# Two-layer diffusion trunk step on one core: expert weights loaded during the output projection, a fused last choice in the router's tail, gathers that read their list directly, and unread matrix products in TensorE's waits

## The reference

```python
x = post_norm(x, concat([ya, yb, yc]) @ w_out[l], g_a, ln_g[l, 0], ln_b[l, 0])
h = x * (1.0 + sc_f) + sh_f
x = post_norm(x, moe_ffn(h, w_router_grp[l], w_router_exp[l], w_e_gate[l], w_e_up[l], w_e_down[l]),
              g_f, ln_g[l, 1], ln_b[l, 1])
# moe_ffn: the group with the largest of 4 logits, in it the 2 largest of 8 expert logits,
# y = sum over the two of weight * ((silu(h @ w_g[e]) * (h @ w_u[e])) @ w_d[e]), 32 experts in all
```

## Time and profile before

| | us |
|---|---|
| median of 3 runs (1667.3 to 1669.96) | 1669.04 |
| the profiled execution | 1667.84 |
| its span | 1666.0 |
| PE busy in the span | 1448.5 |
| DVE busy in the span | 617.1 |
| POOL busy in the span | 391.9 |

### The profile page before, as it was taken

How to read it: one execution, slowest core, us unless ns; L and a number is a source line. 1 busy time by engine, 2 the same in 40 slices (tenths; PEclk the granted TensorE clock), 3 DMA queues, 4 the chain that set the end, 5 groups by cost and what they waited for, 6 DMA issues and landing times.

```text
span 1666.0 us, 23079 instructions
## 1 busy us (share of the span) xinstructions
PE 1448.5 (87%) x8501; PEld 997.3 (60%) x8501; DVE 617.1 (37%) x1454; ACT 351.7 (21%) x908; POOL 391.9 (24%) x537
## 2 busy tenths in 40 slices
PE   6999999997993899897799999999697569899764
PEld 4889889675882333342288989967477434333321
DVE  1301333765458121111351133466728742121116
ACT  2111112654000111111141121156400101111103
POOL 1000032623534111111110001453256221211110
PEclk8999999999995999999899999999998779999987
DMA  9321112875209899999621111176130679999954
GB/s 368 96 69 61 35 56 74 285 260 197 91 26 377 326 369 421 396 412 361 250 85 61 60 61 61 35 276 241 40 127 26 265 286 382 415 413 420 383 226 163
DMA packets 75758, 356.26 MB, mean 214 GB/s; under 512 B 21152, under 2 KB 24480, under 8 KB 40832
## 3 DMA queue, kind: packets, MB, share of 16 engines
q1 hardware_dynamic: 41184, 291.58, 44.5%
q0 software_dynamic: 21888, 48.83, 8.2%
q10 hardware_dynamic: 12576, 14.37, 2.6%
HBM read 344.37 MB, written 33.12 MB: 227 GB/s over the span
## 4 chain that ended last, share of the span: by engine, by line
PE 70%; DMA 18%; DVE 5%; issue 3%; POOL 2%; ACT 1%; SPq 1%; ACTq 0%; POOLq 0%; DVEq 0%
PE bank L978 24%; PE bank L1319 11%; DMA att<-h_rows,cur 9%; PE bank L1204 7%; PE bank L1338 4%; DMA ring<-in_w_exp 4%; PE bank L727 2%; PE bank L758 2%; PE bank L1303 2%; PE bank L1130 2%; PE bank L1104 2%; DMA z<-in_w_ada 1%; PE bank L742 1%; PE bank L935 1%; DMA att<-bias_full 1%
## 5 line engine op out<-in xcount | busy, mean ns | idle before, releaser
L978 PE MATMUL bank<-ring,hT 128*128 128x256 f32 (+1 forms) x1920 | 411.4, 374 | 2.4 <-ACT hT L1430 2.4
L978 PEld LDWEIGHTS bank<-ring,hT 128*128 128x128 f32 x1920 | 353.3, 191 | 47.4 <-issue 2.9
L1319 PE MATMUL bank<-ring,att 128*64 128x512 f32 (+1 forms) x448 | 186.3, 647 | 3.3 <-DMA z<-in_w_exp 3.3
L1319 PE MATMUL bank<-z,att 128*64 128x512 f32 (+1 forms) x416 | 164.2, 618 | 16.0 <-DMA ring<-in_w_exp 16.0
L1204 PE MATMUL bank<-ring,hT 128*128 128x256 f32 x640 | 145.8, 388 | 7.3 <-DMA ring<-in_w_out 5.8
L1204 PEld LDWEIGHTS bank<-ring,hT 128*128 128x128 f32 x640 | 123.1, 195 | 24.2 <-issue 7.6
L2347 DVE TENSOR_TENSOR att<-att,bank 128x256 f32<-128x256 f32 x38 | 16.0, 421 | 294.9 <-ACT att L1670 294.9
L1319 PEld LDWEIGHTS bank<-ring,att 128*64 128x64 f32 (+1 forms) x448 | 60.7, 162 | 82.1 <-issue 82.1
L1319 PEld LDWEIGHTS bank<-z,att 128*64 128x64 f32 (+1 forms) x416 | 52.7, 151 | 74.7 <-issue 74.7
L2635 POOL COPY cur<-att 128x1 int32<-128x1 int32 (+1 forms) x38 | 6.9, 182 | 377.5 <-ACT att L1677 280.2
L1303 PE MATMUL bank<-const,att 128*128 128x128 f32 x320 | 48.1, 299 | 54.6 <-DMA att<-h_rows,cur 54.6
(11 more groups left out here) (366 smaller groups left out, 2168.9 us busy)
## 6 DMA issues: line engine op xcount, KB each, us to landing
ring<-in_w_exp SPq DMA_DIRECT2D x84, 1024.0 KB, 16.8
z<-in_w_exp SPq DMA_DIRECT2D x78, 1024.0 KB, 17.8
ring<-in_w_ada SPq DMA_DIRECT2D x41, 1024.0 KB, 5.5
ring<-in_w_in SPq DMA_DIRECT2D x24, 1024.0 KB, 4.9
hT<-in_w_exp SPq DMA_DIRECT2D x20, 1024.0 KB, 15.7
att<-in_w_exp SPq DMA_DIRECT2D x10, 1024.0 KB, 14.8
z<-expert_rows ACTq DMA_DIRECT2D x20, 512.0 KB, 8.2
ring<-in_w_out SPq DMA_DIRECT2D x8, 1024.0 KB, 8.4
```

What stands on the lines that cost most here:

```text
L978: last = eng.matmul(bk[:, i * UN:i * UN + nw], hTv[:, k, t * P:(t + 1) * P], w[:, k, 0:nw], start=(k == 0), stop=(k == KD - 1))
L1319: last = eng.matmul(bank[2 + j][c * m_:(c + 1) * m_, :], e["xT"][:, j, k * P + c * m_:k * P + (c + 1) * m_], wv[c][:, :, k, :], start=(k = ...
```

## The change

- **Loads.** SP loads the four first experts in twelve pieces. Five are issued at `ld_scsh`, when the projection has begun: the ring slots that held no unit of w_out, and three parts of `z` that nothing uses. The four slots of w_out follow as they come free, two pieces come after the last residual, one after the last logits. Before it waits for `ctl`, SP now waits until the gathers 0 and 1 have landed. The rows `ln2` take the place of `free` in `z`, and GpSimd's temporary moves to `hs`.
- **Projection.** `project` waits for each unit of w_out on its own instead of for all four.
- **Router's tail.** `choose_last` replaces `choose(1)` for the single last tile, with the compare fused with its multiply: 15 instructions up to `assign`, not 19, and the two that feed ACT come after it. DVE adds the shift to the last two tiles (`rows_shifted`). ACT clears `xg`. `ranks(0)` moves ahead of the last transposes.
- **Gathers.** In the fixed passes the gather takes its column of `gidx` itself, without the copy to `cur` and the wait for it; in pass 0 gate and up come before the transposes of pass 1, on all three engines.
- **Unread products.** `keep_busy(n)` issues n products of 128 by 128 by 128 that nothing reads, at four places: 16, 26, 22 and 36 in each layer.

Waits between DVE's own instructions in `choose_last` and the reordered passes of ACT and DVE are left out below.

```diff
--- before.py
+++ after.py
@@ -458,14 +458,13 @@
-            ("ln", P, 2, D), ("free", P, 2, D), ("ga", P, 2, D)])
+            ("ln", P, 2, D), ("ln2", P, 2, D), ("ga", P, 2, D)])
...
-        m["ln2"] = region(z, 2048 + 3 * KD * UN, P, 2, D)
@@ -662,18 +661,29 @@
-                for n in range(2):
-                    for q in range(3):
-                        eng.wait_ge(*ev.at(*holder[3 * n + q]))
-                    gate_up(n, lambda q: A["w_exp"][l, n, q])
-                    down(n, lambda q: A["w_exp"][l, n, q])
+                def piece(n, q):
+                    into, landed = (wdn[n], f"wd{n}") if q == 2 else (wgu[n][:, q, :], f"wgu{n}")
+                    eng.dma_start(into, A["w_exp"][l, n, q]).then_inc(W[landed], 16)
+
+                with_out = [s for s in range(RING) if holder[s][2] == "out"]
+                eng.wait_ge(*ev.at("ld_scsh", l))
+                for s in range(RING):
+                    if s not in with_out:
+                        eng.wait_ge(*ev.at(*holder[s]))
+                        piece(s // 3, s % 3)
+                for n, q in ((2, 2), (3, 0), (3, 1)):
+                    piece(n, q)
+                for s in with_out:
+                    eng.wait_ge(*ev.at(*holder[s]))
+                    piece(s // 3, s % 3)
                 eng.wait_ge(*ev.at("u", l, NT - 1))
                 eng.wait_ge(*ev.at("rows", l))
-                for n in range(2, 4):
-                    if n == 3:
-                        eng.wait_ge(*ev.at("full", jobs.number(("RL", l, NT - 1))))
-                    gate_up(n, lambda q: A["w_exp"][l, n, q])
-                    down(n, lambda q: A["w_exp"][l, n, q])
+                piece(2, 0)
+                piece(2, 1)
+                eng.wait_ge(*ev.at("full", jobs.number(("RL", l, NT - 1))))
+                piece(3, 2)
+                for j in range(2):
+                    eng.wait_ge(W[f"gath{j}"], 16)
                 eng.wait_ge(*ev.at("ctl", l))
@@ -747,6 +757,11 @@
+            def keep_busy(n):
+                for _ in range(n):
+                    eng.matmul(ada_ps[:, 0:P], ident, K["ones"], start=True, stop=True)
@@ -1197,8 +1212,11 @@
-                w = [unit_view((l, "out", u)) for u in range(N_OUT)]
+                w = {}
                 def project(t, half, i):
+                    if t == 0:
+                        w[2 * half + i] = unit_view((l, "out", 2 * half + i))
                     bk = jobs.bank("Y", l, t, half)
@@ -1261,9 +1279,11 @@
+                ranks(0)
                 rows_turned(NT - 1)
-                ranks(0)
                 logits(NT - 1)
+                eng.wait_ge(*(ev.at("hcol", l + 1) if l + 1 < DEPTH else ev.at("modT", l, 1)))
+                keep_busy(16)
                 ranks(1)
@@ -1277,6 +1297,7 @@
+                keep_busy(26)
                 bk = jobs.open("RX", l)
@@ -1349,15 +1370,21 @@
                 def one_pass(b_):
-                    block_x(b_ + 1)
-                    block_gu(b_)
+                    if isinstance(b_, int) and b_ == 0:
+                        block_gu(b_)
+                        block_x(b_ + 1)
+                    else:
+                        block_x(b_ + 1)
+                        block_gu(b_)
                     if above_zero(b_):
                         block_down(b_ - 1)
                     block_hT(b_)
+                keep_busy(22)
                 block_x(0)
                 n = passes(eng, l, one_pass)
                 block_down(n - 1)
+                keep_busy(36)
@@ -1652,6 +1679,12 @@
+                for t in range(NT):
+                    eng.wait_ge(*ev.at("st_h2", l, t))
+                eng.wait_ge(*ev.at("assign", l, 1))
+                for j in range(2):
+                    last = eng.activation(e["xg"][:, j, :].rearrange("p (k n) -> p k n", k=KD), bc(K["ones"], 1, KD), ACT.Copy, scale=0.0)
+                last.then_inc(*act.event("nought", l))
 
                 W = MOE[l]
...
@@ -2132,6 +2169,10 @@
+                def rows_shifted(t):
+                    hs = lr["hs"][:, t % 2, :]
+                    eng.tensor_tensor(hs, hs, lr["scsh"][:, 1, min(t, 1), :], ALU.add).then_inc(*dve.event("h2", l, t))
+
@@ -2181,6 +2222,46 @@
+                def choose_last():
+                    part, t = 1, NT - 1
+                    col = lambda i: s5[:, i, t:t + 1]
+                    lg, le = r["lg"][:, t, 0:NG], r["lg"][:, t, NG:36].rearrange("p (g e) -> p g e", g=NG)
+                    tg, th, lem, hit = r["tg"][:, t, :], r["th"][:, t, :], r["lem"][:, t, :], r["t1"][:, t, :]
+                    eng.wait_ge(*jobs.empty("RL", l, t))
+                    eng.tensor_reduce(col(0), lg, AX, ALU.max).then_inc(*dve.step())
+                    eng.scalar_tensor_tensor(out=th, in0=lg, scalar=col(0), in1=K["io4"], op0=ALU.is_equal,
+                                             op1=ALU.mult).then_inc(*dve.step())
+                    eng.tensor_reduce(col(1), th, AX, ALU.max).then_inc(*dve.step())
+                    eng.tensor_scalar(th, th, col(1), -1.0, ALU.is_equal, ALU.add).then_inc(*dve.step())
+                    eng.scalar_tensor_tensor(out=lem.rearrange("p (g e) -> p g e", g=NG), in0=bc(th, 2, EPG), scalar=-NEG, in1=le,
+                                             op0=ALU.mult, op1=ALU.add).then_inc(*dve.step())
+                    def top(val, one):
+                        eng.tensor_reduce(val, lem, AX, ALU.max).then_inc(*dve.step())
+                        eng.scalar_tensor_tensor(out=hit, in0=lem, scalar=val, in1=K["io32"], op0=ALU.is_equal,
+                                                 op1=ALU.mult).then_inc(*dve.step())
+                        eng.tensor_reduce(col(5), hit, AX, ALU.max).then_inc(*dve.step())
+                        eng.tensor_scalar(one, hit, col(5), None, ALU.is_equal).then_inc(*dve.step())
+
+                    top(col(3), r["e1"][:, t, :])
+                    eng.scalar_tensor_tensor(out=lem, in0=r["e1"][:, t, :], scalar=2 * NEG, in1=lem, op0=ALU.mult,
+                                             op1=ALU.add).then_inc(*dve.step())
+                    top(col(4), r["e2"][:, t, :])
+                    eng.tensor_tensor(r["ma"][:, t, :], r["e1"][:, t, :], r["e2"][:, t, :], ALU.add).then_inc(*dve.event("assign", l, part))
+                    eng.tensor_scalar(tg, lg, col(0), None, ALU.subtract).then_inc(*dve.event("r_gd", l, part))
+                    eng.tensor_tensor(col(6), col(4), col(3), ALU.subtract).then_inc(*dve.event("r_dl", l, part))
@@ -2218,8 +2299,9 @@
                 expert_rows(NT - 2)
+                rows_shifted(NT - 2)
                 logit_rows(NT - 1)
-                choose(1)
+                choose_last()
                 expert_rows(NT - 1)
@@ -2241,6 +2323,7 @@
                 eng.tensor_reduce(kr[0:NE, 5, 0:1], kr[0:NE, 4, :], AX, ALU.add).then_inc(*dve.event("place", l))
+                rows_shifted(NT - 1)
                 bk = jobs.bank("RB", l)
                 eng.wait_ge(*jobs.full("RB", l))
...
@@ -2572,18 +2659,19 @@
                 eng.wait_ge(*ev.at("ld_scsh", l))
                 eng.wait_ge(*ev.at("ld_ln", 1, l))
                 for g in range(2):
-                    eng.tensor_tensor(m["free"][:, g, :], lr["scsh"][:, 0, g, :], m["ln"][:, 1, :], ALU.mult).then_inc(*pool.step())
+                    eng.tensor_tensor(lr["hs"][:, g, :], lr["scsh"][:, 0, g, :], m["ln"][:, 1, :], ALU.mult).then_inc(*pool.step())
                     eng.wait_ge(*pool.last())
-                    eng.tensor_tensor(lr["scsh"][:, 1, g, :], lr["scsh"][:, 1, g, :], m["free"][:, g, :], ALU.add)
+                    eng.tensor_tensor(lr["scsh"][:, 1, g, :], lr["scsh"][:, 1, g, :], lr["hs"][:, g, :], ALU.add)
                     last = eng.tensor_tensor(lr["scsh"][:, 0, g, :], lr["scsh"][:, 0, g, :], m["ln"][:, 0, :], ALU.mult)
                 last.then_inc(*pool.event("rows", l))
                 eng.wait_ge(*pool.last())
                 def store_rows(t):
-                    eng.wait_ge(*ev.at("hsc", l, t))
                     hs = lr["hs"][:, t % 2, :]
-                    eng.tensor_tensor(hs, hs, lr["scsh"][:, 1, min(t, 1), :], ALU.add).then_inc(*pool.event("h2", l, t))
-                    eng.wait_ge(*pool.last())
+                    if t < NT - 2:
+                        eng.wait_ge(*ev.at("hsc", l, t))
+                        eng.tensor_tensor(hs, hs, lr["scsh"][:, 1, min(t, 1), :], ALU.add).then_inc(*pool.event("h2", l, t))
+                    eng.wait_ge(*ev.at("h2", l, t))
                     ld(h2_dram[l][t * P:(t + 1) * P, :], hs, "st_h2", l, t, sem=f"st_h2_{t % 2}")
                 for t in range(NT):
@@ -2598,10 +2686,7 @@
                 store_rows(NT - 1)
                 for t in range(NT):
                     eng.wait_ge(*ev.at("st_h2", l, t))
-                eng.wait_ge(*ev.at("assign", l, 1))
-                eng.memset(e["xg"][:, 0, :], 0.0)
-                eng.memset(e["xg"][:, 1, :], 0.0).then_inc(*pool.step())
```

(10 more changed lines are left out.)

26 lines of the change are left out of this document (22 added, 4 removed).

## The result

The changed kernel takes 1654.9 us, the median of 6 runs (1649.17 to 1660.58), beside 1668.71 for the kernel before (6 runs, 1665.38 to 1672.75): a ratio of 0.9918, 95% interval 0.9902 to 0.9935. That is 13.8 us faster, inside the range and on the forecast side, but only half of the 28.0 us of the sum. The profiled execution of after took 1653.13 us with a span of 1651.3, and its mean granted clock rose from 0.933 to 0.953.

A forecast was written before the change was run, and what follows sets the result against it. The prediction took the stream of expert weights, started by the end of pass 0's gate and up, to set the pace. Terms 3.6 + 7.9 + 9.2 + 2.2 + 2.1 + 3.0 = 28.0 us gave 1641, range 1628 to 1657.

The forecast's parts named there:

- the moment: End of gate and up of pass 0, which starts the full weight stream; forecast 7.9 us earlier, 9.2 in layer 1.
- Projection: Start of layer 0's projection: a wait per unit of w_out brings 3.6 us, bounds 0 and 4.9; layer 1 nothing.
- The collision priced at 449.2: Layer 0's projection: transposes of tile 1 near 449.2, not 447.8, where the second residual meets GpSimd's add.
- Steps 1 to 5: Router's tail, logits to lists: shift +0.7, choice 1.3 earlier, comparison 2.7 earlier, second shift +0.3, list products 2.5 us.
- Step 6: First gather, without copy and wait, issues near 526.6; rows land 5.0 us later, transposes of pass 0 end at 532.6.
- Step 7: DVE's readout of pass 0's transposes, late through two GpSimd adds, comes at 537.0; gate and up start at 537.8.
- Step 8: Gate and up of pass 0, now ahead of pass 1's transposes, still take 8.3 us and end at 546.2.
- The stream: Expert passes behind the moment: move as a block, with 1.5 us a layer gained, bounds 0 and 6.
- Combination: Combination behind the expert passes, no longer started cold: 2.2 us in layer 0, 2.1 in layer 1, bounds 0 and 2.5.
- part of the gain is absorbed: Rival: projection's start brings 0, tail 5 a layer through new DVE and GpSimd collisions, combination waits: 1656, chance 0.22.
- Bound by the gather's latency: Rival: the expert passes are bound by gather latency, not bytes, giving 6 us a layer, not 1.5: 1632, chance 0.2.
- The slower rival: Rival: unread products run at 1.2 GHz, 0.24 us each, deciding from about 0.19 us an instruction: 1683, chance 0.05.

The follow-up runs named there:

- run 9: The kernel before, unaltered, timed and profiled again: 1667.78 us, ratio 0.9995.
- Run 4: The changed kernel with the copy to `cur` and its wait restored ahead of every gather: 1658.35 us, ratio 0.9935.
- run 5: The changed kernel with GpSimd's two layer norm additions and the loads behind them moved behind gather 2: 1643.61 us, ratio 0.9833.
- Run 7: The changed kernel with 18 more unread products behind the transposes of pass 0: 1652.38 us, ratio 0.9895.
- run 1: The changed kernel again, with no edit: 1654.62 us, ratio 0.992.
- run 3: The changed kernel with the twelve weight pieces loaded after the last projection, as before, and without SP's wait for the gathers: 1653.7 us, ratio 0.991.
- run 6: The changed kernel with GpSimd's two additions behind gather 2, and 20 and 14 unread products for 26 and 22: 1641.23 us, ratio 0.9841.
- runs 8 and 11: Changed kernel with pass 0's old order, 1656.31 us; changed kernel with GpSimd's additions behind gather 2, early loads and SP's gather wait undone, 1651.88 us.

## Why the prediction was half right

The direction and the place were right: the gain comes through the moment, and from there the work moves as a block (252.26 and 252.83 us before, 252.21 and 252.72 after). Its steps against the rows, in us from the end of layer 0's logits (505.1 in the working, 505.62 after):

| step | before | forecast | after |
|---|---|---|---|
| 2, `assign` | 5.7 | 4.4 | 4.8 |
| 3, counts compared | 9.4 | 6.7 | 6.8 |
| 4, list products start | 20.0 | 17.7 | 17.7 |
| 5, lists | 25.5 | 21.3 | 21.0 |
| 6, transposes of pass 0 end | 34.1 | 27.5 | 28.8 |
| 7, gate and up start | 40.7 | 32.7 | 33.3 |
| 8, gate and up end | 49.0 | 41.1 | 42.9 |

- **Projection.** The forecast gave 3.6 us; to the transposes of tile 1 the means of run 9 give 42.1 less 38.7, 3.4. The collision priced at 449.2 in the text came. The failed part is "behind it TensorE is without a gap, so the shift holds": in the 3.91 us of wait that the step left out TensorE loses its clock, and 2.2 us (94.5 less 92.3) reach the logits, 1.8 by the mean of eleven profiles. Run 4's profile shows what the clock costs: there the wait was 2.97 us, the granted clock stayed at 1.00 over the 7 us behind it (0.76 in after), and the stretch took 90.0, 4.5 less than before. Of the 2.4 us by which it beats after, the shorter wait is 0.9. In run 5's profile the clock was 0.56 over these 7 us, the last logits took 2.91 us instead of 1.95, and nothing was gained (95.0).
- **Steps 1 to 5** hold within 0.4 us. The second shift fits into the sums' wait, at 0, not 0.3. No stall is left in the choice and the comparison takes 0.18 us. The rule on VectorE and GpSimd that the prediction cites from the Trainium skill ("SBUF — State Buffer", section "Who interferes with whom") agrees with the rows outside the choice as well: with the additions moved, 3.71 and 2.30 us became 0.87 and 0.17.
- **Step 6** was 1.3 off, since the 22 unread products end at 533.5, not 531.0 (0.154 us each, not 0.13, and started at 526.8; the granted clock was 0.50 from 528 to 530). It cost nothing, VectorE being later still.
- **Step 7** named the collision and sized it 0.6 too small.
- **Step 8** failed in its mechanism: "they still take 8.3 us". They took 9.65 and 9.79 where 8.29 and 8.89 had stood before. The text took the colder start as priced by the row of before. There, transposes of 1.97 us stand directly ahead of gate and up and take the first of the slow time: the granted clock is 0.50 in the first 2 us of gate and up and 0.88 in the next two. After, gate and up come straight from 4.49 us of idle and have 0.50 for all four. Run 7 shows the clock as cause, since unread products in that wait bring 7.09. The size varies: gate and up behind cold transposes, with the old order of pass 0, took 7.6 to 9.2 us in eight cases. Steps 7 and 8 together leave 6.0 and 7.1 of the 7.9 and 9.2 (the terms of the 9.2 add up to 9.3).
- **The stream.** "The gather's missing copy" was to give 1.5 a layer, and gives nothing measurable: the lengths above, and run 4 in layer 1. This is the largest single term that failed, 3.0 of the 28.0 us. That a gather issued 1 us sooner waits for the same bytes is argued from the full DMA share; in part the rows agree, since from issue to landing the median gather of a window of 220 us takes 10.2 us with the copies (before, and run 4 in layer 1) and 10.5 and 10.8 without (after, run 1).
- **Combination.** 2.3 and 2.1 us by the rows of the combination; forecast 2.2 and 2.1. That both came out is partly luck. In the ten profiles with the 36 unread products, seven of twenty combinations took 12.2 us (layer 0) or 19.1 (layer 1), since the granted clock fell after their start, as in run 5, layer 0, combination from 808.24 on:

```profile
810.24:812.24 2.00, 2.00 (x4) 0.68 (x3) 1.35 (x2) 0.00 (x0) 0.00 (x0) 0.50 1.03 412
```

The terms as measured are 2.2 + 6.0 + 7.1 + 0 + 2.3 + 2.1 = 19.7 us, against 28.0. Of the 8.3 us that are missing, 3.0 are the stream's, 4.0 those of steps 6 to 8 and 1.4 the projection's; the combination gave 0.1 more than forecast. The spans of the two profiles of each kernel (1666.0 and 1664.7; 1651.3 and 1644.8) differ by 17.3 in the mean, the medians by 13.8 and 15.5. The two profiles of the changed kernel are of executions faster than its median. In the first pair of profiles, what stands between the 19.7 and the 14.7 of the spans lies mostly in attention, which the change doesn't touch: it took some 3 us more in each layer. Beyond that: runs of the changed kernel spread over 16 us, those of before over nearly 9, and the time goes with the granted clock (0.954 in runs of 1646.6 and 1649.2 us, 0.947 in runs of 1660.6 and 1662.7). Without unread products the spread is 3.3 us (five runs), but run 3, which has them, spreads over 4.2. Where clock is lost in some executions the profiles show in part: at the start of a combination (seven of twenty, 1.7 us each), in the list products (three of eighteen, 2.0 us each) and behind the wait in the projection. Why it is lost there in some executions and not in others stays open, and so does what is left between 19.7 and 13.8.

Of the rivals, "part of the gain is absorbed" (1656) came true in size, and in half of its mechanism: VectorE and GpSimd do collide anew, and moving GpSimd's additions brings 11 us. The tail didn't fall to 5 a layer nor did the combination wait. "Bound by the gather's latency" is refuted by the streams. The slower rival's condition held for part of two groups (granted clock 0.50), but no group came to its 0.19 us an instruction: they took 0.12 to 0.17 in the two profiles of the changed kernel, and without them the kernel is 5.3 us slower.

What the prediction missed most was the reach of its own step 7. It took the additions as given, "in both versions", and so did not ask what they cost once their cover was gone. Their price is 0 in the kernel before, 11 us in the changed one, and 1.8, which the intervals don't tell from none, with the loads as before.

## What to carry to other kernels

When a change removes the wait that ended last, list what else ended inside it: here two GpSimd additions of 2.4 us, free before, cost 11 us after, and the early loads for which the change was made paid (8 us) only when these were moved. Two edits that bring nothing by themselves can bring something together, so cross them. GpSimd additions that VectorE's small instructions have to sit out belong behind the gather that the critical chain needs next, not in front of it. Price a burst of TensorE by the granted clock at its start, not by its own former duration: the same 32 instructions took 7.09 to 9.87 us. The wait directly ahead isn't enough to tell that clock: after 4.49 us it was low, but in run 3 also after 0.92, behind short transposes and a longer wait.

## What the runs showed of the hardware

- VectorE instructions of one element or five columns last as long as the GpSimd addition of 128x1024 beside them (3.71 for five, 2.30 for one; 0.87 and 0.17 without it). All that an addition stretched have two tensors in SBUF as inputs. Instructions with one such input stood beside an addition too and weren't stretched. In the kernel before, the reduction directly ahead of the 4-column subtraction that took 1.34 us lies inside the same addition and takes its 0.16:

```profile
504.71 2.34 POOL L2585 TENSOR_TENSOR att<-att 128x1024 f32<-128x1024 f32 x1 [1.88 <-DVE att L2131]
505.54 0.16 DVE L2148 TENSOR_REDUCE small<-att 128x1 f32<-128x4 f32 x1
```

The same goes for an input in SBUF with one in PSUM: 0.68 us for the addition of 128x512 from a bank at 448.88 of after, beside GpSimd's addition of 447.79.

- Unread products bring the clock back, but don't keep it from falling. In after an instruction takes 0.119 us directly behind the logits, 0.165 over the 52 (granted clock 0.50 from 514 to 520), 0.154 over the 44 (0.50 from 528 to 530), 0.115 over the 72 behind the last down products. In three of eighteen cases (run 6 layer 1, runs 8 and 11 layer 0) the group ahead of the list products ran at full clock, 0.117 to 0.118 us, and so ended 2.4 to 3.8 us early, and the clock fell behind it: the list products took 4.33 or 4.34 us, as with no unread products at all (4.45).
- The first gather of run 6, issued at 524.94, had its rows there at 529.6, 4.6 us later. Issued 3.2 us behind two expert pieces, as gather 2 of run 4, it took 11 us and cost TensorE 7.5. Why run 5's, issued at 537.93 just ahead of such pieces, didn't, was not tested apart.
